# Gates of two mixer branches as seven block products for eight, with all spatial products in the first gate pair

## What is computed

```
mq, mk, mv, mo, mi, mf, su, sv, wq, wk, wv, gl = split_in(h @ p['w_in'])
...
z = jnp.einsum('gpr,bnrgc->bnpgc', w, vc) + b_s[:, :L].T[None, None, :, :, None]
return u * z.reshape(B, S, SG_W), vn
...
gates = jax.nn.sigmoid(gl).reshape(B, S, N_BRANCH, D_MODEL)
merged = (gates[:, :, 0] * (y_ml @ p['w_br_mlstm'])
          + gates[:, :, 1] * (y_sg @ p['w_br_gmlp'])
          + gates[:, :, 2] * (y_sw @ p['w_br_swa']))
x = x + g1 * rms_norm(merged @ p['w_out'], p['g_post_mix'])
```

## Time and profile before

| What | Value |
|---|---|
| median of 3 runs | 2061.83 us |
| the profiled execution | 2064.86 us, of it a span of 2063.1 us |
| TensorE matmul busy | 2030.5 us, 98% of the span |
| TensorE weight load busy | 1959.7 us, 95% |
| VectorE | 987.8 us, 48% |
| ScalarE | 624.9 us, 30% |
| GpSimd | 1064.4 us, 52% |
| granted TensorE clock | 0.998 of full |

### The profile page before, as it was taken

How to read it: one execution, slowest core, us unless ns; L and a number is a source line. 1 busy time by engine, 2 the same in 40 slices (tenths; PEclk the granted TensorE clock), 3 DMA queues, 4 the chain that set the end, 5 groups by cost and what they waited for, 6 DMA issues and landing times.

```text
span 2063.1 us, 38507 instructions
## 1 busy us (share of the span) xinstructions
PE 2030.5 (98%) x16241; PEld 1959.7 (95%) x16241; DVE 987.8 (48%) x1645; ACT 624.9 (30%) x1358; POOL 1064.4 (52%) x562
## 2 busy tenths in 40 slices
PE   8999999999999999999999999999999999999998
PEld 6998898999999999999999989889999999999997
DVE  5223466422257535647563235663223573647473
ACT  4111224110134333425532121340102343525253
POOL 0443454567763745363734534546687546354543
PEclk9999999999999999999999999999999999999999
DMA  9746232233351333233535342222233413232332
GB/s 358 259 137 52 63 82 59 68 83 86 90 182 42 126 121 92 83 92 93 174 121 174 62 63 76 62 59 75 82 103 89 148 43 91 82 89 85 94 93 77
DMA packets 299771, 211.93 MB, mean 103 GB/s; under 512 B 13728, under 2 KB 293840, under 8 KB 296400
## 3 DMA queue, kind: packets, MB, share of 16 engines
q1 hardware_dynamic: 292848, 205.94, 34.8%
q10 hardware_dynamic: 6752, 3.53, 0.7%
HBM read 204.65 MB, written 4.07 MB: 101 GB/s over the span
## 4 chain that ended last, share of the span: by engine, by line
PE 93%; DMA 2%; DVE 2%; POOL 1%; ACT 1%; issue 1%; SPq 0%; DVEq 0%; POOLq 0%; ACTq 0%
PE ps L971 43%; PE ps L1063 19%; PE ps L999 13%; PE ps L1083 3%; DMA raw<-in_w_in 2%; PE ps L1089 2%; PE ps L1216 2%; PE ps L1131 1%; PE ps L1595 1%; PE ps L1558 1%; PE ps L1573 1%; PE ps L1431 1%; PE ps L1259 1%; PE ps L1110 1%; PE ps L1446 1%
## 5 line engine op out<-in xcount | busy, mean ns | idle before, releaser
L971 PE MATMUL ps<-h_hi,hi_lo 128*128 128x288 f32 x3008 | 541.8, 298 | 1.7 <-POOL hi_lo L885 1.5
L882 POOL TENSOR_TENSOR hi_lo<-raw,consts 128x1024 fp32r<-128x1024 f32 (+1 forms) x124 | 236.8, 1910 | 473.6 <-PE ps L971 354.6
L971 PEld LDWEIGHTS ps<-h_hi,hi_lo 128*128 128x128 f32 x3008 | 446.9, 189 | 9.1 <-issue 5.1
L971 PE MATMUL ps<-h_lo,hi_lo 128*128 128x288 f32 x1504 | 322.2, 296 | 0.0
L885 POOL TENSOR_TENSOR hi_lo<-raw,hi_lo 128x1024 fp32r<-128x1024 f32 (+1 forms) x124 | 300.1, 2420 | 9.7
L898 POOL TENSOR_TENSOR a_lo<-raw,a_hi 128x512 fp32r<-128x512 f32 x108 | 159.2, 1474 | 271.5 <-ACT a_hi L2138 271.4
L971 PEld LDWEIGHTS ps<-h_lo,hi_lo 128*128 128x128 f32 x1504 | 242.6, 189 | 0.0
L999 PE MATMUL ps<-yf_hi,fo_h 128*128 128x288 f32 x704 | 152.5, 298 | 3.0 <-DVE yf_lo L2313 3.0
L1899 ACT ACTIVATE tmp<-ps 128x576 f32<-128x576 f32 x60 | 39.1, 652 | 382.3 <-PE ps L971 382.3
L882 POOL TENSOR_TENSOR hx<-raw,consts 128x1024 fp32r<-128x1024 f32 x34 | 68.4, 2010 | 160.3 <-PE ps L1089 65.1
L999 PE MATMUL ps<-yf_hi,fo_l 128*128 128x288 f32 x704 | 151.0, 296 | 0.0
(11 more groups left out here) (398 smaller groups left out, 4554.5 us busy)
## 6 DMA issues: line engine op xcount, KB each, us to landing
raw<-in_w_in SPq DMA_DIRECT2D x108, 512.0 KB
ada<-in_w_ada SPq DMA_DIRECT2D x23, 2048.0 KB, 8.9
raw<-in_w_ffn_in SPq DMA_DIRECT2D x144, 256.0 KB, 3.1
raw<-in_w_ffn_out SPq DMA_DIRECT2D x32, 384.0 KB
raw<-in_w_ffn_out SPq DMA_DIRECT2D x32, 320.0 KB
raw<-in_w_out SPq DMA_DIRECT2D x16, 512.0 KB
raw<-in_w_ffn_in SPq DMA_DIRECT2D x16, 512.0 KB
raw<-in_w_br_mlstm SPq DMA_DIRECT2D x8, 512.0 KB
```

The lines of the kernel that those rows point to most:

```text
L882: pool.tensor_tensor(hi, RAW[s][:, 0:size], ONES[:, 0:1].to_broadcast([128, size]), ALU.mult).then_inc(chunk_hi, 1)
L971: m = pe.matmul(o[:, h, :], a[:, k, c0:c0 + 128], mv(k, h), start=(k == 0 and begins), stop=(k == nk - 1 and a is wl))
```

## The change

The gates of the last two pairs of branch 1 and of all four pairs of branch 2 (six pairs a layer) are computed as seven block products, as the FFN does. The first two pairs of branch 1 stay as they were. All four spatial products go into the first pair of branch 1: z0 and z1 before br1_0 and br1_1, z2 and z3 behind them.

The data sums t1 to t4 are made once a layer, from h, during the second plain pair: eight additions or subtractions of 128 x 1152 on VectorE (`whole`, `less`), four high parts on ScalarE (`gt_high`), four low parts on VectorE (`gt_low`). t3 takes the place of one block of h. For each gate pair p (0 to 5) the weights come as four blocks of 256 KB (`gate_block`; a11 and a12 into RAW[0], a21 and a22 into RAW[1]), and the branch weights of the pair go into one of the two buffers after its blocks have been read (`gate_branch`). The sums s1, s2 and s4 of a pair share one PSUM bank, the second of the unit `ga{p}` in whose first bank the products run; so s2 is made when the low part of s1 is done. `gate_keep(0, p)` writes over the first gate tile of the pair before, and waits until both tiles of that pair are merged. Matmuls fall from 14914 to 14770; VectorE has 1789 instructions instead of 1645, ScalarE 1456 instead of 1316, GpSimd 550 instead of 562; SyncE issues 461 transfers instead of 437.

```diff
+PLAIN1 = 2
+GPAIRS = [(1, n) for n in range(2 * PLAIN1, 8, 2)] + [(2, n) for n in range(0, 8, 2)]
+NGP = len(GPAIRS)
+Z_AFTER, Z_LATE = {0: (0, 1)}, {0: (2, 3)}
...
+if (_b_, _n) in GPAIRS:
+    _p = GPAIRS.index((_b_, _n))
+    MIX += [f"ga{_p}", f"gb{_p}"]
+    if (_b_, _n) == (2, 6):
+        MIX += [f"br2_{_i}" for _i in range(4, 8)]
+    elif (_b_, _n) != (2, 4):
+        MIX += [f"br{_b_}_{_n}", f"br{_b_}_{_n + 1}"]
+    continue
...
+def gate_blocks_read(o, n):
+    if o != "a21":
+        sp.wait_ge(g_alo, 3 * n + {"a11": 1, "a12": 2, "a22": 3}[o])
+    sp.wait_ge(g_sum, 4 * n + (4 if o == "a12" else 3))
+def gate_block(o, p, g, n, pos):
+    t, k0 = int(o[1] == "2"), 4 * (o[2] == "2")
+    if (BRANCHES[2][1], n) == (g, 6):
+        gate_blocks_read(o, l * NGP + p - 1)
+    else:
+        if p:
+            gate_blocks_read(o, l * NGP + p - 1)
+        sp.wait_ge(chunk_split, split_count(l, pos - 1 if (pos - 1) % 2 == t else pos - 2))
+    sp.dma_start(RAWB[o].rearrange("p (k c) -> p k c", k=4),
+                 w_in[:, k0:k0 + 4, ds(C_GL + g * D + (n + t) * 128, 128)]).then_inc(g_raw[o], 16)
+def gate_branch(pos, p, w_br, n):
+    for o in ("a21", "a22") if pos % 2 else ("a11", "a12"):
+        gate_blocks_read(o, l * NGP + p)
+    load(pos % 2, pos, RAW[pos % 2][:, 0:1024].rearrange("p (k c) -> p k c", k=4),
+         w_br[:, :, ds(n * 128, 256)])
...
+for pos in range(4 * (l == 0), PAIR_AT[GPAIRS[0]]):
+    split(pos)
+for p, (b, n) in enumerate(GPAIRS):
+    for o in ("a11", "a12", "a22"):
+        gate_block_lo(o, p)
+    if (b, n) != (2, 4):
+        for pos in range(PAIR_AT[b, n] - ((b, n) == (2, 6)), PAIR_AT[b, n] + 1):
+            split(pos)
+for pos in range(P_WO, P_FO):
...
+def gate_begins(p, x):
+    n = l * NGP + p
+    if x == "p1":
+        pe.wait_ge(unit_of(l, f"ga{p}"), empty(l, f"ga{p}"))
+        pe.wait_ge(g_alo, 3 * n + 1)
+    elif x == "p5":
+        pe.wait_ge(unit_of(l, f"gb{p}"), empty(l, f"gb{p}"))
+        pe.wait_ge(g_lo, 4 * n + 1)
+        if p == 0:
+            pe.wait_ge(gt_lo, nth(gt_lo, l, 0))
+    elif x == "p6":
+        pe.wait_ge(g_lo, 4 * n + 2)
+        pe.wait_ge(g_kept, 3 * n + 1)
+        if p == 0:
+            pe.wait_ge(gt_lo, nth(gt_lo, l, 1))
+    elif x == "p2":
+        pe.wait_ge(g_alo, 3 * n + 2)
+    elif x == "p7":
+        pe.wait_ge(g_lo, 4 * n + 3)
+        pe.wait_ge(g_kept, 3 * n + 3)
+        if p == 0:
+            pe.wait_ge(gt_lo, nth(gt_lo, l, 3))
+    elif x == "p3":
+        pe.wait_ge(g_lo, 4 * n + 4)
+    else:
+        pe.wait_ge(g_alo, 3 * n + 3)
+        pe.wait_ge(g_c22, n + 1)
+def gate_pair(p):
+    gate_begins(p, "p1")
+    for i, x in enumerate(PRODUCTS):
+        wh, wl = GOPND[WEIGHTS[x]]
+        bh, bl = DATA[x]
+        o = gate_rest(l, p)[:, x != "p2", :] if x in ("p2", "p5", "p3") else gate_chain(l, p)
+        for k in range(4):
+            for a, mv in ((wh, bh), (wh, bl), (wl, bh)):
+                if k == 3 and a is wl and i < 6:
+                    gate_begins(p, PRODUCTS[i + 1])
+                m = pe.matmul(o, a[:, k * 128:(k + 1) * 128], mv(k), skip_group_check=True,
+                              start=(k == 0 and mv is bh and a is wh and x in ("p1", "p5", "p2")),
+                              stop=(k == 3 and a is wl))
+        m.then_inc(g_prod, 1)
...
+def gt_high(i, dst, src):
+    act.wait_ge(gt_sum, nth(gt_sum, l, (2, 5, 7, 4)[i]))
+    act.activation(dst, src, ACT.Copy).then_inc(gt_hi, 1)
+def gate_block_high(o, p):
+    n = l * NGP + p
+    act.wait_ge(g_raw[o], 16 * (n + 1))
+    if p:
+        act.wait_ge(g_prod, gate_product(n - 1, {"a11": "p1", "a12": "p2", "a22": "p4"}[o]))
+    act.activation(GOPND[o][0][:, :], RAWB[o], ACT.Copy).then_inc(g_ahi, 1)
+def gate_sum_high(i, p):
+    n = l * NGP + p
+    act.wait_ge(g_sum, 4 * n + i)
+    if p:
+        act.wait_ge(g_prod, gate_product(n - 1, {1: "p5", 2: "p6", 3: "p7", 4: "p3"}[i]))
+    act.activation(GOPND[f"s{i}"][0][:, :], GS3SUM[:, :] if i == 3 else gate_sum(l, p), ACT.Copy) \
+       .then_inc(g_hi, 1)
...
+def gate_keep(i, p):
+    n = l * NGP + p
+    first, second = GTILES[p]
+    act.wait_ge(g_prod, gate_product(n, ("p1", "p5", "p6")[i]))
+    if i == 0 and GPAIRS[p] != (2, 6):
+        b, m = GPAIRS[p][0], GPAIRS[p][1] - 2
+        if m < 0:
+            b, m = b - 1, 6
+        for e in range(2):
+            act.wait_ge(unit_of(l, f"br{b}_{m + e}"), read(l, f"br{b}_{m + e}"))
+    dst = (first[:, 0:HALF], second[:, HALF:T], first[:, HALF:T])[i]
+    act.activation(dst, gate_rest(l, p)[:, 1, :] if i == 1 else gate_chain(l, p), ACT.Copy).then_inc(g_kept, 1)
...
+                for n in range(0, 2 * PLAIN1, 2):
                     gate(1, n)
-                    z_bias(g)
+                    if n == 0:
+                        z_bias(0)
+                    else:
+                        gt_high(0, T1H[:, :, :], T1SUM[:, :, :])
                     gate(1, n + 1)
-                    act.wait_ge(unit_of(l, f"z{g}"), read(l, f"z{g}"))
-                    y_hi(4 + g, WQ[:, 2 + g % 2, :])
-
-                for n in range(2):
-                    act.wait_ge(unit_of(l, f"br1_{n + 6}"), read(l, f"br1_{n + 6}"))
-                for n in range(8):
-                    if n < 6:
-                        act.wait_ge(merged2, before(merged2, l, n))
-                    tile(f"g2_{n}", TS[:, n % 2, :] if n < 6 else SQ[:, n - 6, :], ACT.Tanh, 0.5)
+                    if n == 0:
+                        z_bias(1)
+                        for g in range(4):
+                            act.wait_ge(unit_of(l, f"z{g}"), read(l, f"z{g}"))
+                            y_hi(4 + g, WQ[:, 2 + g % 2, :])
+                            if g < 2:
+                                z_bias(2 + g)
+                gt_high(1, T2H[:, :, :], T2SUM[:, :, :])
+                gt_high(2, T4H[:, :, :], T4SUM[:, :, :])
+                gt_high(3, T3H, GT3SUM[:, :, :])
+                act.wait_ge(o_stored, l * (16 * O_STORES) + 16 * O_STORES)
+                for o in ("a11", "a12"):
+                    gate_block_high(o, 0)
+                for i in (1, 2, 3):
+                    gate_sum_high(i, 0)
+                gate_block_high("a22", 0)
+                gate_sum_high(4, 0)
+                for p, bn in enumerate(GPAIRS):
+                    close = bn == (2, 4)
+                    gate_keep(0, p)
...
+def gt_low(i, lo, total, hi):
+    dve.wait_ge(gt_sum, nth(gt_sum, l, 7))
+    dve.wait_ge(gt_hi, nth(gt_hi, l, i))
+    tt(lo, total, hi.bitcast(f32), ALU.subtract).then_inc(gt_lo, 1)
+def gate_weights(i, p):
+    n, bank = l * NGP + p, gate_sum(l, p)
+    if i == 1:
+        dve.wait_ge(g_raw["a21"], 16 * (n + 1))
+        dve.wait_ge(g_raw["a22"], 16 * (n + 1))
+        dve.wait_ge(unit_of(l, f"ga{p}"), empty(l, f"ga{p}"))
+        x = bank, RAWB["a21"], RAWB["a22"], ALU.add
+    elif i == 2:
+        dve.wait_ge(g_raw["a11"], 16 * (n + 1))
+        dve.wait_ge(g_lo, 4 * n + 1)
+        x = bank, bank, RAWB["a11"], ALU.subtract
+    elif i == 3:
+        if p:
+            dve.wait_ge(g_prod, gate_product(n - 1, "p7"))
+        x = GS3SUM[:, :], RAWB["a11"], RAWB["a21"], ALU.subtract
+    else:
+        dve.wait_ge(g_raw["a12"], 16 * (n + 1))
+        dve.wait_ge(g_lo, 4 * n + 2)
+        x = bank, RAWB["a12"], bank, ALU.subtract
+    tt(*x).then_inc(g_sum, 1)
+def gate_weights_low(i, p):
+    dve.wait_ge(g_hi, 4 * (l * NGP + p) + i)
+    hi, lo = GOPND[f"s{i}"]
+    tt(lo[:, :], GS3SUM[:, :] if i == 3 else gate_sum(l, p), hi[:, :].bitcast(f32), ALU.subtract).then_inc(g_lo, 1)
...
+for n in range(0, 2 * PLAIN1, 2):
+    for g in Z_AFTER.get(n, ()):
+        spatial_gate(g)
+    if n == 2:
+        whole(0, GT3SUM[:, :, :], 0, 1)
+        whole(1, T1SUM[:, :, :], 0, 0)
+        less(2, T1SUM[:, :, :], GT3SUM[:, :, :], T1SUM[:, :, :])
+    merge(1, n)
+    if n == 2:
+        whole(3, T2SUM[:, :, :], 1, 1)
+        less(4, GT3SUM[:, :, :], T2SUM[:, :, :], GT3SUM[:, :, :])
+    merge(1, n + 1)
+    for g in Z_LATE.get(n, ()):
+        spatial_gate(g)
+    if n == 2:
+        less(5, T2SUM[:, :, :], T2SUM[:, :, :], T1SUM[:, :, :])
+        whole(6, T4SUM[:, :, :], 1, 0)
+        less(7, T4SUM[:, :, :], T4SUM[:, :, :], T2SUM[:, :, :])
+        gt_low(0, T1L[:, :, :], T1SUM[:, :, :], T1H[:, :, :])
+        gt_low(1, T2L[:, :, :], T2SUM[:, :, :], T2H[:, :, :])
+gt_low(2, T4L[:, :, :], T4SUM[:, :, :], T4H[:, :, :])
+gate_weights(1, 0)
+gate_weights_low(1, 0)
+gt_low(3, T3L, GT3SUM[:, :, :], T3H)
+gate_weights(2, 0)
+gate_weights_low(2, 0)
+gate_weights(3, 0)
+gate_weights(4, 0)
+gate_weights_low(3, 0)
+gate_weights_low(4, 0)
+for p, (b, n) in enumerate(GPAIRS):
+    if (b, n) == (2, 4):
+        gate_weights(1, p + 1)
+        gate_weights_low(1, p + 1)
+        gate_weights(2, p + 1)
+        gate_weights_low(2, p + 1)
+        gate_c22(p)
+        gate_weights(3, p + 1)
+        gate_first(p)
+        gate_weights(4, p + 1)
+        gate_weights_low(3, p + 1)
```

(16 more changed lines are left out.)

204 lines of the change are left out of this document (147 added, 57 removed).

## The result

| | before | after |
|---|---|---|
| median of 4 runs | 2061.59 us (2060.82 to 2062.76) | 2110.49 us (2107.89 to 2113.33) |
| the profiled execution | 2064.86 us, span 2063.1 | 2112.81 us, span 2110.8 |
| granted TensorE clock, mean | 0.998 | 0.982 |

The ratio is 1.0237, interval 1.0219 to 1.0255, 48.9 us between the medians. It lies inside the stated range of 2077 to 2114, 9.5 us above the predicted 2101 and above the 2089 to 2108 of the prediction's likeliest case. The four runs of the change fall in two pairs, 2107.9 and 2108.2 us at a mean granted clock of 0.987 to 0.988, 2112.8 and 2113.3 us at 0.982 to 0.983; the profile is of the longer pair.

What follows compares the result with a forecast made beforehand. The prediction took TensorE's list of matmuls as the bound. Waits of 29.6 us a layer less 9.9 saved make 19.7 more, 39.4 in two layers; against 2061.83 us it gave 2101 us, range 2077 to 2114.

Steps and rivals of the forecast that it cites:

- likeliest case: Whole kernel: waits outweigh the saved matmuls, with no charge for a lower clock; 2101 us, 2089 to 2108, chance 0.59.
- The saving: Gate products on TensorE: a pair takes 11.15 us instead of 12.80, 1.65 us less; six pairs in two layers, 19.8 us.
- z1: Spatial product z1: its bias stands on ScalarE behind the tanh of g1_1, so it begins some 0.3 us late.
- p1 of pair 0: First gate pair: TensorE stands from 453.0 to 465.1 us, 12.2 us, until GpSimd's low part of a11 ends.
- the walk: Layer 0 followed operation by operation from 408.4 us, using traced durations; it puts the end of br1_3 at 453.0 us.
- p5 and p6 of pair 0: First gate pair: p5 waits 0.5 us for s1, p6 4.5 us for the copy `gate_keep(0)`, which ends at 473.2.
- p6 of pairs 1 to 4: Later pairs: merges, copy and late blocks make p6 wait 1.9, 3.9, 0.8 and 4.0 us.
- p7 of pair 4: Pair 4: keep(2) stands behind the sums of pair 5, so p7 waits 1.6 us.
- busy matmul time about 19 us less: Sign in the profile after the change: TensorE's busy matmul time falls by about 19 us.
- The clock falls too: Rival: TensorE's clock drops behind long stops, 9.5 us charged; 2111 us, 2105 to 2120, chance 0.17.
- a clock row below full at 23 and 72% of the span: Sign of the clock's rival: clock below 1.0 in those slices, with products of more than 1.59 us.
- Its price: Charge for the lower clock: one product of 1.59 us at twice its length for each of six stops, 9.5 us.

Runs made afterwards that it cites:

- e_two: The edits of e_own, e_sums and e_merge together, pair 4's third copy and pair 0's weight sums earlier, against the changed kernel; 2072.95 us, ratio 1.0053.
- e_sums: Against the changed kernel, VectorE makes all eight data sums ahead of the merges of br1_2 and br1_3; 2105.12 us, ratio 1.0208.
- e_four: Against the changed kernel, gate pairs only in branch 2, four a layer, with data sums spread over three plain pairs; 2088.39 us, ratio 1.0121.
- e_warm: Against the changed kernel, dummy matmuls in TensorE's stops at p1 of pair 0 and p6 of pairs 0 to 4; 2106.75 us, ratio 1.0218.
- e_own: Against the changed kernel, branch weights of pairs 1 to 3 get a buffer of their own; 2096.13 us, ratio 1.0162.
- e_alt: Against the changed kernel, gate tiles of the pairs alternate between two buffers; 2104.97 us, ratio 1.0204.
- e_four_all: e_four plus own branch-weight buffer, merges ahead of s3 and s4, and the first pair's s1, s2 ahead of the last merges; 2070.49 us, ratio 1.0042.
- e_four_best: e_four_all plus the last but one pair's copies ahead of the last pair's a11 high part, and s1's low part behind br1_6's merge; 2069.01 us, ratio 1.0026.
- e_merge: Against the changed kernel, both merges ahead of s3 and s4, and the first copy ahead of s3's high part; 2123.21 us, ratio 1.0297.

## Why the prediction held, and where it did not

- **The saving.** Forecast 1.65 us a pair. Pairs without a stop take 11.12 us in e_two, 11.15 forecast. Right.
- **z1.** Forecast 0.3 us, measured 0.32 in each layer. Right.
- **p1 of pair 0.** Forecast 12.2 us, measured 11.70: br1_3 ended at 453.84 us for 453.0 in the walk, and p1 began at 465.54 for 465.1. e_sums and e_four show its cause, the data parts on VectorE and ScalarE. Right. (12.2, 0.5 and 4.5 make 17.2, not the 17.1 that the sum uses.)
- **p5 and p6 of pair 0.** Forecast 0.5 + 4.5 us with p6 at 473.2 us; p6 started at 473.20 and TensorE stood only 1.81 us. The other 2.6 us are p1 and p5 at the 1.2 GHz level (24 matmuls at 0.24 for 0.133 us). The prediction said that a slow clock costs nothing there; e_warm, where p6 comes 7.75 us after p1 instead of 7.66, shows it.
- **p6 of pairs 1 to 4.** Forecast 1.9, 3.9, 0.8, 4.0 us; measured 1.98, 3.93, 1.14, 3.94 in layer 0 and 1.02, 3.81, 1.28, 3.94 in layer 1. Both causes hold for pairs 2 and 4: e_own removes their excess over the others (the loads), and in e_two, which has the other order of the merges among its edits, the remaining 1.15 us is gone from pairs 2 to 4. Of late blocks in pairs 1 and 3 only one case shows: in layer 0 ScalarE waited 0.85 us for a12 of pair 1. In pair 1 of layer 1 and in pair 3 it took a11 and a12 without a wait, and pair 3 stands 1.15 us in e_own as well, so what is left for its stop is the order of the merges.
- **p7 of pair 4.** Forecast 1.6 us, measured 0.26 and less. The slow matmuls before it used up the time: with the clock up it is 1.38 in e_warm, and 1.71 in e_own, where the stop before it is short.
- **The clock.** Here the forecast erred. My likeliest case had none of it, and its sign "busy matmul time about 19 us less" failed: it is 0.4 us more. The rival "The clock falls too" had 0.17 and gave 2111 us; 2110.49 was measured, and by its own sign, a clock row below full at 23 and 72% of the span, it is what happened. Its ground was in the earlier trace rows already: the clock fell some 4 us after TensorE's last record, and a stop of 12 us could not have left it up. I took the absence of a row at the lower level for a reason to leave the charge out, when such a row was missing only because nothing had ever stopped.
- **Its price.** I charged 9.5 us for six stops at twice the length of one product. Measured are 20.2 us more matmul time, of which 2.6 us at p5 and p6 and 1.4 at p7 in each layer stand in place of forecast stops: 12.2 us against 9.5. One stop that I had not charged is among them, the 1.98 us at p6 of pair 1 in layer 0, with 1.8 us of slow matmuls behind it. Yet keeping the clock up returned some 3.7 us of time in e_warm. Part of the rest was cover for the loads: pair 3 alone gave back 1.2 us. The price as an account and the price as an intervention differ by that much, and the second is the one that an edit gets.

So the waits were forecast at 29.6 us a layer and stood 24.6, nearly all of the difference taken by the slow clock in front of them, and the sum came out by a term that the likeliest case had at nothing. The time fell into the stated range because that range was drawn over the clock's rival as well; the likeliest case alone ends 2.5 us below it. The clock rival's 2111 came out so near for two reasons. Over both layers its waits were 10.0 us too high and its charge for the clock 10.7 us too low, and 8.0 us of that is one time under two names, the slow matmuls in place of stops. The rest, 2.0 too high against 2.7 too low, cancelled by luck.

## What to carry to other kernels

A product that is saved on the bound engine is worth its time only if each preparation stands early enough in its engine's list, and ahead of anything that waits for a transfer; here 1.65 us a pair stood against stops of 1 to 12, and the same idea with five pairs, an own buffer and another order gained 7 us of the 16.5 that its shorter list had to give. When a stop goes and comes back two products later, look for the second queue that the same late load holds. And a stop costs more than itself when the clock falls behind it: give the clock a term of its own in the sum, not a case beside it.

## What the runs showed of the hardware

- The granted clock's fall can come late and land wholly in work. In pair 1 of layer 0 TensorE stood 1.98 us before 494.46, and the stretches around it (columns as above) are:

```profile
490.00:495.00 5.00, 3.02 (x23) 2.81 (x23) 4.26 (x7) 2.17 (x5) 1.27 (x1) 1.00 0.04 4
495.00:500.00 5.00, 5.00 (x28) 5.00 (x27) 0.00 (x0) 0.70 (x2) 2.70 (x2) 0.66 0.67 205
```

  The same followed stops of 2.31 (pair 2 of layer 0 in e_alt) and 2.38 us (pair 0 of e_four_all). Each of the three pairs took some 1.75 us more than 11.15 and its stop; behind the 3.93 us of pair 2 it is 2.4. Behind stops of 1.02 to 1.60 us (pair 1 of layer 1 and pair 3 of layer 0 in the change, pair 0 of e_four_best) it is 0.2. The length of the stop alone doesn't decide it: pair 2 of layer 1 in e_merge stood 1.80 us and took 1.74 us more, while pair 3 of layer 0 there stood 2.70 us and took 0.4 more, at a full clock:

```profile
531.00:533.50 2.50, 0.04 (x1) 0.00 (x0) 2.34 (x6) 0.32 (x1) 0.00 (x0) 1.00 0.00 0
533.50:535.00 1.50, 1.27 (x9) 1.30 (x10) 1.41 (x3) 1.26 (x4) 0.00 (x0) 1.00 0.00 0
535.00:537.00 2.00, 2.00 (x18) 2.00 (x17) 0.87 (x2) 1.15 (x3) 1.30 (x1) 1.00 0.00 0
```

  The Trainium skill ("TensorE: Matmul & The Clock Gate", Part 1) speaks of an idle engine whose clock falls; the trace agrees, and shows that it fell while the engine was busy again.
- At the 0.50 reading matmuls of 288 columns follow each other every 0.24 us against 0.133, 1.8 times as long, not twice.
- VectorE's 128x1152 sum and GpSimd's split lengthen each other: 3.55 for 1.35 us and 3.40 for 2.4 where they ran side by side in e_sums. Of the 6.9 us by which p1 came earlier there, 3.3 were left at p6.
